# The low part of the weights last: a strip's half in three runs of eight products

## What is computed

```python
for layer in range(DEPTH):                      # DEPTH = 2
    hp, hs = _rmsnorm(xp, gn[0]), _rmsnorm(xs, gn[0])
    if layer % 2 == 0:
        mp, rows_p, sw_p = _ab_prompt(hp, ..., w_in_mix[e], w_out_mix[e], attn_sinks[e])
        ms, rows_s, sw_s = _ab_sample(hs, ..., w_in_mix[e], w_out_mix[e], attn_sinks[e])
    else:
        mp, st_p = _ret_mixer(hp, ..., w_in_ret[o], w_out_ret[o])
        ms, st_s = _ret_mixer(hs, ..., w_in_ret[o], w_out_ret[o])
    xp = xp + _rmsnorm(mp, gn[1])               # the same for xs
    xp = xp + _rmsnorm(_mlp(_rmsnorm(xp, gn[2]), w_ff1[layer], w_ff2[layer]), gn[3])

def _mlp(h, w1, w2):
    a = jax.nn.relu(h @ w1)
    return (a * a) @ w2
```

## Time and profile before

| | us |
|---|---|
| median of 3 runs | 1023.28 (1023.24 to 1023.64) |
| the profiled execution | 1023.53 |
| its span, first to last instruction | 1021.7 |
| TensorE busy | 985.4 (96%) |
| VectorE busy | 601.0 (59%) |
| ScalarE busy | 436.8 (43%) |
| mean granted TensorE clock | 0.994 of full speed |

### The profile page before, as it was taken

One profiled execution on the slowest core, in us unless ns is written; L12 is line 12 of the kernel. 1 busy time (PEld: TensorE's weight loads), 2 busy tenths in 40 slices (PEclk: granted clock), 3 DMA queues, 4 the chain that ended last, 5 costly groups with the idle time before them and its releaser, 6 DMA issues. The chain is left out here.

```text
span 1021.7 us, 17488 instructions
## 1 busy us (share of the span) xinstructions
PE 985.4 (96%) x7438; PEld 899.1 (88%) x7438; DVE 601.0 (59%) x744; ACT 436.8 (43%) x552; POOL 33.4 (3%) x68
## 2 busy tenths in 40 slices
PE   6999999989999999999999999999999999999995
PEld 6888999655899999999997878779799999999995
DVE  6766554547378554334685676577573785553344
ACT  5322323556555554333443362625344554443331
POOL 0310000000000000000000000000100000000000
PEclk9999999999999999999999999999999999999998
DMA  9887859735525444444544958675764254444421
GB/s 358 306 281 256 286 163 343 268 124 185 228 93 176 174 170 166 168 169 170 202 173 146 365 188 287 251 266 207 266 248 168 92 195 165 164 165 167 164 80 46
DMA packets 50701, 206.62 MB, mean 202 GB/s; under 512 B 3536, under 2 KB 3920, under 8 KB 35024
## 3 DMA queue, kind: packets, MB, share of 16 engines
q1 hardware_dynamic: 45216, 182.58, 50.8%
q0 software_dynamic: 5424, 23.15, 5.8%
HBM read 181.39 MB, written 24.33 MB: 201 GB/s over the span
## 5 line engine op out<-in xcount | busy, mean ns | idle before, releaser
L575 PE MATMUL banks<-hH,wH 128*128 128x288 f32 x1248 | 377.7, 303 | 17.0 <-DVE hL L1545 13.0
L1170 ACT ACTIVATE wH<-raw 128x2048 fp32r<-128x2048 f32 x116 | 222.3, 1916 | 368.8 <-PE banks L577 366.6
L1536 DVE TENSOR_TENSOR wL<-raw,wH 128x2048 fp32r<-128x2048 f32 x113 | 258.9, 2291 | 192.8 <-ACT wH L1170 192.5
L576 PE MATMUL banks<-hL,wH 128*128 128x288 f32 x1248 | 369.8, 296 | 0.0
L577 PE MATMUL banks<-hH,wL 128*128 128x288 f32 x1248 | 369.8, 296 | 0.0
L575 PEld LDWEIGHTS banks<-hH,wH 128*128 128x128 f32 x1248 | 237.6, 190 | 35.5 <-issue 22.5
L576 PEld LDWEIGHTS banks<-hL,wH 128*128 128x128 f32 x1248 | 236.9, 190 | 0.4
L577 PEld LDWEIGHTS banks<-hH,wL 128*128 128x128 f32 x1248 | 236.5, 189 | 0.0
L576 PE MATMUL banks<-aL,wH 128*128 128x288 f32 x512 | 151.0, 295 | 0.0
L577 PE MATMUL banks<-aH,wL 128*128 128x288 f32 x512 | 150.9, 295 | 0.0
L575 PE MATMUL banks<-aH,wH 128*128 128x288 f32 x512 | 150.2, 293 | 0.0
(11 more groups left out here) (265 smaller groups left out, 1031.2 us busy)
## 6 DMA issues: line engine op xcount, KB each, us to landing
raw<-wst SPq DMA_DIRECT2D x120, 1024.0 KB, 4.9
cache_sb<-kcache SPq DMA_DIRECT2D x14, 1024.0 KB, 5.9
sslot<-state SPq DMA_DIRECT2D x11, 1024.0 KB, 6.9
sstate_out<-sslot POOLq DMA_DIRECT2D x11, 1024.0 KB, 6.5
raw<-vcache SPq DMA_DIRECT2D x6, 1024.0 KB, 9.6
w_area<-vcache SPq DMA_DIRECT2D x6, 1024.0 KB, 13.0
raw<-state SPq DMA_DIRECT2D x5, 1024.0 KB, 7.2
sstate_out<-raw POOLq DMA_DIRECT2D x5, 1024.0 KB, 5.6
```

Source lines behind the costliest of these rows:

```text
L575: nc.tensor.matmul(out[:, m, :], wH[:, u % 2, c], hi[:, k, :], start=first, stop=False)
L576: nc.tensor.matmul(out[:, m, :], wH[:, u % 2, c], lo[:, k, :], start=False, stop=False)
L1170: nc.scalar.activation(wH[:, at % SPL, :], raw[:, raw_slot(at), :], ACT.Copy).then_inc(h_round, 1)
L1536: nc.vector.tensor_tensor(wL[:, at % SPL, :], raw[:, raw_slot(at), :], wH[:, at % SPL, :].bitcast(F32), ALU.subtract).then_inc(l_split, 1)
```

## The change

In product() the three matmuls of a tile no longer stand together. For each half m: eight matmuls on wH with the high activations, eight on wH with the low ones, then eight on wL with the high ones. The wait at the front asks for the rounded weights (h_round) instead of the split ones, and the wait for l_split stands before the first run on wL, in the first half only. For the first of the four strips of a down output (kq = 0) the front wait stays l_split: there the split, which VectorE issues behind its evacuation, also tells that the PSUM pair is free. tile_product stays for the other callers. strip_used and half_used are raised by the last matmul of the strip and of the first half, as before.

```diff
-            def product(s, u, out, hi, lo, start=True, stop=True, half=False):
-
-                pe.wait_ge(l_split, s + 1)
+            def product(s, u, out, hi, lo, start=True, stop=True, half=False, free=True):
+
+                pe.wait_ge(h_round if free else l_split, s + 1)
                 for m in range(2):
+
+                    for part in (hi, lo):
+                        for k in range(KT):
+                            c = slice(k * SC + m * P, k * SC + m * P + P)
+                            nc.tensor.matmul(out[:, m, :], wH[:, u % 2, c], part[:, k, :],
+                                             start=start and k == 0 and part is hi, stop=False)
+                    if m == 0:
+                        pe.wait_ge(l_split, s + 1)
                     for k in range(KT):
-                        mm = tile_product(u, out, hi, lo, m, k, start, stop)
-                        if half and (m, k) == (0, KT - 1):
-                            mm.then_inc(half_used, 1)
+                        c = slice(k * SC + m * P, k * SC + m * P + P)
+                        mm = nc.tensor.matmul(out[:, m, :], wL[:, u % 2, c], hi[:, k, :], start=False, stop=stop and k == KT - 1)
+                    if half and m == 0:
+                        mm.then_inc(half_used, 1)
                 mm.then_inc(strip_used, 1)
...
-                                aL[:, 8 * kq:8 * kq + 8, :], start=kq == 0, stop=kq == 3, half=u == 7)
+                                aL[:, 8 * kq:8 * kq + 8, :], start=kq == 0, stop=kq == 3, half=u == 7, free=kq > 0)
```

## The result

| | before | after |
|---|---|---|
| median of the paired runs, us | 1023.55 | 1025.93 |
| ratio after to before | | 1.0027 (95%: 1.0018 to 1.0036) |
| the profiled execution, us | 1023.53 | 1025.92 |
| its span, us | 1021.7 | 1024.1 |
| mean granted TensorE clock | 0.994 | 0.993 |

The forecast was 1025.6 us, out of a slower step. The page of the kernel after: first busy time by engine, and then two of the groups of matmuls (line, engine, names, count; busy us, mean ns; idle us ahead of them and who ended most of it). Line 570 issues both runs on wH in product(), line 576 the run on wL, line 584 is tile_product, which the other loops still use.

What follows compares the result with a forecast made beforehand. TensorE, without idle time in the MLP products, was taken as the bound, so the step between matmuls counts: 2.0 us for h products plus 0.3 for a and y gives 1025.6 us against 1023.28; own range 1024.0 to 1027.6, overall down to 1021.0.

Steps and rivals of the forecast that it cites:

- No product waits for the split: The 88 products through product(): moving the split's wait behind 16 matmuls gains 0, at most 0.7 us.
- The added wait costs nothing: Second wait inside each of 88 products: met by over 3 us, so 0; 0.11 us each as the other end.
- A restart at each: Rival, at the 88 added waits: each keeps next weights from loading ahead, 0.11 us each, 9.7 us, 1033.0 us; chance 0.05.
- A changed order gives a slower step for the h products: 50 products with h operands, 2400 steps: 132.25 instead of 131.4 ns, 2.0 us more; slower step's chance 0.45.
- the nearest row: first_strips: sixteen wL products in a row with h operands, 132.5 ns a step, taken as closest to the new order.
- The a and y products, +0.3 us: 32 down products and 6 of the retention's output, 1824 steps: from 132.2 to at most 132.5 ns, 0.3 us taken.
- The sum: Whole kernel: 2.0 us for h products plus 0.3 for a and y products, together 2.3 us, giving 1025.6 us.
- The indifferent order: Rival, the matmul step: set by the 288 columns and where tiles lie, so nothing changes, 1023.3 us; chance 0.25.
- The quicker order: Rival, h products: runs of eight bring all steps to 130.0 ns, 3.4 us less, 1019.9 us; chance 0.17.
- saved split wait: Rival, product starts: some wait for the split today, so the change gives at most 0.7 us, 1022.6 us; chance 0.08.

Runs made afterwards that it cites:

- e2: Kernel before, in its order, with the change's front wait and the split's wait ahead of the first wL matmul: 1023.33 us, ratio 1.0004.
- m1: Small kernel, TensorE alone, series of 96 matmuls in varied orders and pitches; at 292 words 131.6 ns a step in the order of before, 132.6 after.
- m3: Small kernel, TensorE alone, one tile read over and over at sixteen start addresses, plus some series at aH's and other places: 130.1 to 134.6 ns a step.
- e1: Kernel after with the single wait for the split at the front again, so the order alone: 1025.89 us, ratio 1.0028.
- e3: Kernel before with rows of hH and hL at a pitch of 288 words instead of 292: 1028.01 us, ratio 1.0054.
- e4: Kernel after with rows of hH and hL at a pitch of 288 words instead of 292: 1028.06 us, ratio 1.0046.
- e7: Kernel after with hH and hL moved by 16 words in SBUF: 1024.79 us, ratio 1.0018 to the kernel before.
- e8: Kernel before with hH and hL moved by 16 words in SBUF: 1024.74 us, ratio 1.0019.
- e6: Kernel after with rows of aH and aL at a pitch of 292 words: 1025.80 us, ratio 1.0028; thirteen down strips 82.25 us.
- e5: Kernel before with rows of aH and aL at a pitch of 292 words: 1023.17 us, ratio 1.0004; thirteen down strips 82.43 us.
- m2: Small kernel, TensorE alone, pitch 292, moving operand shifted by 0 to 28 words, both orders: 131.6 to 132.5 ns before, 131.6 to 132.5 after.

## Why the prediction was right, and where it was off

**No product waits for the split: right.** The tightest case is still the retention's output, and it answers to the earlier trace rows. The timeline, VectorE's split and TensorE's runs:

```profile
764.58 2.28 DVE L1545 TENSOR_TENSOR wL<-raw,wH 128x2048 fp32r<-128x2048 f32 x1
...
768.26 1.22 PE L570 MATMUL banks<-yH,wH 128*128 128x288 f32 x8
...
770.37 0.82 PE L576 MATMUL banks<-yH,wL 128*128 128x288 f32 x5
```

The split ends at 766.86. It was ready 1.40 us ahead of the product's start, as before, and is now ready 3.51 us ahead of its first use; the forecast had 3.5 or more. e2 confirms the price of zero.

**The added wait costs nothing: right.** From the last matmul ahead of it to the first behind it are at most 0.13 us in the profile after, but for the one strip at the half clock (0.24). In the half shown above the run ahead of the wait takes 1.05 us from start to start, no more than its neighbours. A restart at each would have given 9.7 us. e2, with the same wait at another point, measures 1.0004.

**A changed order gives a slower step for the h products: right in sign and kind, undersized.** The step of the argument was: each other order of these operands in the trace is slower than today's, 132.0 to 133.0 ns, so take 132.25. Measured were 132.8 ns in the up strips, 1.4 above 131.4, and on average over all 2400 steps 2.98 us / 2400 = 1.24 ns, against 0.85. What failed is the choice within the range: I took the wL run of first_strips for the nearest row. The third run of a half is indeed like it, 132 ns (132.5 there), and the second is quicker, 131; but the first, hH on wH behind another run on hH, takes 135 ns, as lines 161 and 162 of m1 have it, and no row of before shows such a run. The end of the range, 133.0, did cover the mean. The premise, that another order of these operands is a slower one, holds for this layout and not in general: 16 words further on, and for aH and aL at a pitch of 292, the same new order is the quicker one. The sign came out right because the rows it was taken from have the same tiles at the same places.

**The a and y products, +0.3 us: not there.** 132.2 ns before and after, and within 0.02 us in 30 down strips. The forecast reckoned with up to 132.5. m3 has this pair by itself: a pitch of 288 words at the place of aH takes 12.69 us in the order of before (269.50 to 282.19) and 12.69 us in that of after (to 294.88), 132.2 ns both.

**The sum.** 2.3 us were forecast, 2.98 us are to be seen in the strips, and 2.4 us in the medians and in the spans. That the forecast hits the median to 0.3 us is partly luck: in the profiles a start 1.16 us earlier hides more than the terms that I missed. The strips' own sum is what to trust, and it lies within the interval of the paired runs (1.8 to 3.7 us).

**The rivals.** The indifferent order is refuted for this layout by e1, but its reason was half right: e3, e4, e7 and e8 show layouts in which it is indifferent, and "where the tiles lie" is what decides the sign. The quicker order is refuted here, and yet exists: e6 against e5, 0.3 ns a step. Its 130.0 ns came from a single 0.39 us read to a hundredth; the three steps of the earlier trace rows together are 1.18 us for nine matmuls, 131.1 ns. The 122.5 ns that the prediction takes from the Trainium skill, "TensorE: Matmul & The Clock Gate", section "Back-to-back issue gap", is an estimate by a formula that this section gives for the isolated gap of a single matmul, so the prediction leaned on it too much as a rule for this stream. No series comes down to it; the lowest is 130.1 ns. Restart and saved split wait are refuted by e2: 88 restarts would be 9.7 us, and its interval runs from 0.6 us less to 1.4 more. The 0.7 us in the list of waits are there after the change too.

**What stays open.** Why a start address gives 130.1 or 134.6 ns, and why the same series takes 132.5 ns at one time and 131.9 at another, isn't known; no run looks inside the read of the moving operand. That it hangs on which words are read as the moving operand is shown (lines 193 and 194 of m1, and m3); that it is a conflict between addresses following each other is only a guess, and the order's effect can't be worked out from m3's table. Open, too, is how much of the medians' differences comes by the clock behind the attention.

## What to carry to other kernels

Before moving a wait, compare each consumer's start with the end of what it waits for: where everything is ready 1.4 us ahead, an earlier start is worth nothing, and a met wait more costs nothing. Where TensorE has no gap, the quantity to compare is the distance from start to start, over whole strips; 1.2 ns in 2400 steps are 3 us, and neither the list of waits nor the idle times show it. Such a step is to be taken anew after each change of order, pitch or address, and a small kernel with nothing but series of matmuls finds most of it; for another layout the result of this change may have the other sign.

## What the runs showed of the hardware that was not expected

- A 128x288 matmul on 128x128 weights at the full clock has no fixed step: 130.1 to 134.6 ns, by the address at which its moving operand starts (m3, TensorE alone, one tile read over and over).
- The step hangs on the order in which moving tiles are read, 131.6 against 132.5 ns at one place and 132.5 against 131.7 at 16 words on (m2), and a run of eight on hH takes 135 ns behind another run on hH and 132 behind one on hL (m1). The same series had 132.5 and 131.9 ns in one execution (m3). Whether the weights change or stay made no difference (m1).
- Behind the attention the granted clock of the same 13 us was 0.74, 0.87 and 1.00 in executions whose work there is nearly the same, with the same order at 0.74 and 1.00. The strip there took 8.58 and 6.43 us with the same order, a difference of 2.15 us between two profiles, as much as the whole change.
